# A two-layer diffusion backbone on one core: one gate job moved to the third feed-forward, the filter network's steps spread from turn 6 on, and two norms turned to columns by scaled x and transposes

## What is computed

```
def modulated_norm(x, g, shift, scale):
    return rms_norm(x, g) * (1 + scale) + shift

def half_step_ffn(x, g_pre, g_post, shift, scale, gate, w_gate, w_up, w_down):
    h = modulated_norm(x, g_pre, shift, scale)
    y = (jax.nn.silu(h @ w_gate) * (h @ w_up)) @ w_down
    return x + FFN_RES * gate * rms_norm(y, g_post)

def hyena_filters(n, w1, b1, w2, b2, w3, b3, w4, freq):
    ...
    hdn = jnp.sin(fr * (z @ w1.astype(f32) + b1.astype(f32)))
    hdn = jnp.sin(fr * (hdn @ w2.astype(f32) + b2.astype(f32)))
    hdn = jnp.sin(fr * (hdn @ w3.astype(f32) + b3.astype(f32)))
    filt = (hdn @ w4.astype(f32)).reshape(n, 2, HY_WIDTH)

def reference(...):
    for i in range(DEPTH):
        m_lat = (jax.nn.silu(c) @ w_mod[i] + b_mod[i]).reshape(b, N_MOD, 1, D_MODEL)
        ...
```

## Time and profile before

| what | value |
|---|---|
| median of 3 runs | 1338.75 us (1336.57 to 1341.46) |
| the profiled execution, its own time | 1343.3 us |
| its span in the trace | 1341.5 us |
| busy PE / DVE / ACT / POOL | 97% / 73% / 47% / 9% |
| mean granted TensorE clock | 0.992 of full speed |
| moved by DMA | 275.12 MB |

### The profile page before, as it was taken

The page is one execution under the profiler, slowest core; times in us unless marked ns, Lnnn a source line. Parts: engine busy times, 40 slices in busy tenths (PEclk is TensorE's granted clock), DMA queues, the critical chain, the costliest instruction groups (busy, mean ns, idle before and its releaser), DMA issues.

```text
span 1341.5 us, 21469 instructions
## 1 busy us (share of the span) xinstructions
PE 1306.6 (97%) x7794; PEld 1125.8 (84%) x7794; DVE 982.1 (73%) x1447; ACT 632.9 (47%) x969; POOL 118.1 (9%) x209
## 2 busy tenths in 40 slices
PE   6899999999999999999999999999999999999997
PEld 3678777887778988789999868999998987989996
DVE  5788777788776776759888778887558797865554
ACT  6632333332376665755444337444447434644443
POOL 3000010111000422011111000110000000000000
PEclk8999999999999999999999989999999999999999
DMA  9555566777655753259888635886653536656652
GB/s 361 186 171 178 199 203 248 254 244 262 227 173 173 204 147 105 79 174 363 292 303 296 198 118 198 309 299 198 189 188 127 158 110 204 236 173 188 183 185 102
DMA packets 76359, 275.12 MB, mean 205 GB/s; under 512 B 9226, under 2 KB 9781, under 8 KB 75712
## 3 DMA queue, kind: packets, MB, share of 16 engines
q1 hardware_dynamic: 52128, 187.00, 42.4%
q0 software_dynamic: 24160, 87.12, 19.0%
HBM read 273.04 MB, written 1.05 MB: 204 GB/s over the span
## 4 chain that ended last, share of the span: by engine, by line
PE 86%; DVE 7%; ACT 3%; DMA 2%; issue 1%; DVEq 0%; SPq 0%; ACTq 0%
PE gu L1671 16%; PE gu L1673 16%; PE gu L1672 16%; PE acc L1732 8%; PE acc L1734 8%; PE acc L1733 8%; DVE wlo_r L1006 2%; PE acc L1721 2%; DMA wlo<-in_wstream_dram 1%; ACT whi L617 1%; PE acc L2017 1%; PE acc L2028 1%; DMA x_lat<-in_x_in_dram 1%; PE acc L1995 1%; PE acc L1996 1%
## 5 line engine op out<-in xcount | busy, mean ns | idle before, releaser
L1671 PE MATMUL gu<-h_hi,whi 128*128 128x256 f32 (+1 forms) x1688 | 518.0, 307 | 4.2 <-DVE h_lo L1131 1.3
L1672 PE MATMUL gu<-h_lo,whi 128*128 128x256 f32 (+1 forms) x1688 | 515.3, 305 | 0.0
L1673 PE MATMUL gu<-h_hi,wlo_r 128*128 128x256 f32 (+1 forms) x1688 | 515.0, 305 | 0.0
L1006 DVE TENSOR_TENSOR wlo_r<-wlo,whi 128x1024 fp32r<-128x1024 f32 x350 | 421.5, 1222 | 100.9 <-ACT whi L617 99.3
L617 ACT ACTIVATE whi<-wlo 128x1024 fp32r<-128x1024 f32 x350 | 360.3, 1049 | 97.8 <-DMA wlo<-in_wstream_dram 97.5
L1671 PEld LDWEIGHTS gu<-h_hi,whi 128*128 128x128 f32 x1688 | 318.8, 189 | 28.6 <-issue 4.0
L1672 PEld LDWEIGHTS gu<-h_lo,whi 128*128 128x128 f32 x1688 | 318.8, 189 | 19.0 <-issue 0.7
L1673 PEld LDWEIGHTS gu<-h_hi,wlo_r 128*128 128x128 f32 x1688 | 319.4, 189 | 15.5
L1023 DVE SCALAR_TENSOR_TENSOR part<-wm,cvec,part 128x512 f32<-128x512 f32 x266 | 199.5, 750 | 6.7
L1732 PE MATMUL acc<-whi,act_hi 128*128 128x512 f32 x440 | 176.7, 402 | 2.5 <-DVE act_lo L1219 2.0
L1734 PE MATMUL acc<-wlo_r,act_hi 128*128 128x512 f32 x440 | 174.9, 397 | 0.0
(11 more groups left out here) (337 smaller groups left out, 1233.2 us busy)
## 6 DMA issues: line engine op xcount, KB each, us to landing
wlo<-in_wstream_dram SPq DMA_DIRECT2D x350, 512.0 KB, 3.6
wm<-in_wmod_dram POOLq DMA_DIRECT2D x132, 512.0 KB, 6.1
area<-in_wmod_dram POOLq DMA_DIRECT2D x11, 512.0 KB, 19.6
z<-in_gate_rows_dram POOLq DMA_DIRECT2D x6, 512.0 KB, 6.7
gate_keep<-in_gate_rows_dram POOLq DMA_DIRECT2D x5, 512.0 KB, 7.1
area<-in_rpb_dram POOLq DMA_DIRECT2D x32, 64.0 KB, 3.6
x_lat<-in_x_in_dram SPq DMA_DIRECT2D x1, 1024.0 KB, 7.5
area<-in_ctx_in_dram SPq DMA_DIRECT2D x1, 1024.0 KB, 8.8
```

Of the source, the lines that this page charges most:

```text
L1006: nc.vector.tensor_tensor(wlo[:, u.base % RING, :], raw[:, u.base % RING, :], whi[:, u.base % RING, :].bitcast(F32), ALU.subtract).then_in ...
L1671: nc.tensor.matmul(out_, w_hi, x_hi, start=start, stop=False, skip_group_check=True)
L1672: nc.tensor.matmul(out_, w_hi, x_lo, start=False, stop=False, skip_group_check=True)
L1673: return nc.tensor.matmul(out_, w_lo, x_hi, start=False, stop=stop, skip_group_check=True)
```

## The change

It has three parts. (1) The two jobs of gate block 2 of layer 1 go from the list of `ffn(1)` to that of `ffn(2)`, with their tile loads on POOL and another slot for a gain. (2) The filter network's steps are set to other places, the first three to turns 6 and 7 instead of 8 and 9, with a table of its own for the sines on ACT; the batch's rows, columns and coefficients move two to four steps back. (3) Norms 3 and 5: DVE scales all of x by 1 / rms into `spare`, PE only transposes, and the columns come one unit later.

```
-        [(1, b, h, LAT) for b in (1, 3, 4, 2) for h in range(2)],
-        [(1, b, h, LAT) for b in (6, 7, 5) for h in range(2)],
+        [(1, b, h, LAT) for b in (1, 3, 4) for h in range(2)],
+        [(1, b, h, LAT) for b in (6, 7, 2, 5) for h in range(2)],
...
-            pool.wait_ge(h_ready, 8 * 5)
-            load_gate(1, 2)
-            load_gain(1, 2)
             with pool.Fori(JOB_L[1] + 1, JOB_L[2] + 1) as l:
                 load_job(l, gemv, steps_before(l))
             pool.wait_ge(h_ready, 8 * 6)
-            load_gate(1, 5)
-            load_gain(1, 5)
+            for b in (2, 5):
+                load_gate(1, b)
+                load_gain(1, b)
...
+                if q in IN_PAIRS:
+                    nc.vector.tensor_scalar(spare[:, t, :], X[NORMS[q][2]][:, t, :], rstd[:, i:i + 1], None,
+                                            ALU.mult).then_inc(diag_done, 1)
+                    return
                 nc.vector.tensor_scalar(diag[:, t, :], ident[:, :], rstd[:, i:i + 1], None, ALU.mult).then_inc(diag_done, 1)
...
+                    if q in IN_PAIRS:
+                        ins = nc.tensor.transpose(columns_of(q, kt)[:, t * P:(t + 1) * P], spare[:, t, kt * P:(kt + 1) * P],
+                                                  ident[:, :])
...
-                if ft == 8:
+                if ft == 9:
...
-                if idx == 8:
+                if idx == 9:
...
-FILTER_AT = [(8, 3), (8, 5), (9, 1), (9, 3), (9, 5), (10, 1), (10, 3)]
+FILTER_AT = [(6, 2), (6, 5), (7, 2), (8, 4), (9, 0), (9, 4), (10, 0)]
+SINE_AT = [(6, 3), (7, 0), (7, 3)]
```

More of the change, by code:

```diff
@@ L75 @@
         + [(l, b, h, LAT) for l, b in ((0, 5), (0, 8), (0, 6), (0, 7), (1, 0)) for h in range(2)],
-        [(1, b, h, LAT) for b in (1, 3, 4, 2) for h in range(2)],
-        [(1, b, h, LAT) for b in (6, 7, 5) for h in range(2)],
+        [(1, b, h, LAT) for b in (1, 3, 4) for h in range(2)],
+        [(1, b, h, LAT) for b in (6, 7, 2, 5) for h in range(2)],
         [(1, 8, h, LAT) for h in range(2)]]
-JOB_0 = [0, 22, 30, 36]
-JOB_L = [AHEAD, 20, 28, 34]
+JOB_0 = [0, 22, 28, 36]
+JOB_L = [AHEAD, 20, 26, 34]
 AHEAD_CHUNKS = 4 * AHEAD
@@ L90 @@
 GATE_JOBS = [job for jobs in JOBS for job in jobs if job[1] in GATE_NORM]
-GATE_SLOT = [0, 1, 0, 0, 0, 0]
+GATE_SLOT = [0, 1, 0, 0, 1, 0]
 COLS_AHEAD = [(0, b, h, s) for b, h in AHEAD_LOADS for s in (LAT, CTX)]
@@ L950, in spectra_norms @@
                 spectrum_out(i + 3)
-            ffn(1, peeled=at_steps([(6, 2)] + FILTER_AT, [lambda: batch_rows(1)] + [lambda l=l: sine(l) for l in range(3)]))
+            ffn(1, peeled=at_steps([(6, 4)] + SINE_AT, [lambda: batch_rows(1)] + [lambda l=l: sine(l) for l in range(3)]))
             load_table(ACT.Sqrt)
@@ L1580, in filter_sums @@
                 assert count[0] == FD_SUM[i]
-            ffn(1, peeled=at_steps([(7, 0)] + FILTER_AT, [lambda: (batch_out(1), norm_coef(9), norm_coef(11))]
+            ffn(1, peeled=at_steps([(7, 4)] + FILTER_AT, [lambda: (batch_out(1), norm_coef(9), norm_coef(11))]
                                    + [lambda l=l: sine_argument(l) for l in range(3)]
@@ L1720, in norm_columns @@
                         pe.wait_ge(xt_copied, kt // 2 + 1)
-                    ins = nc.tensor.matmul(columns_of(q, kt)[:, t * P:(t + 1) * P],
-                                           X[NORMS[q][2]][:, t, kt * P:(kt + 1) * P], diag[:, t, :], start=True, stop=True)
+                    if q in IN_PAIRS:
+                        ins = nc.tensor.transpose(columns_of(q, kt)[:, t * P:(t + 1) * P], spare[:, t, kt * P:(kt + 1) * P],
+                                                  ident[:, :])
+                    else:
+                        ins = nc.tensor.matmul(columns_of(q, kt)[:, t * P:(t + 1) * P],
+                                               X[NORMS[q][2]][:, t, kt * P:(kt + 1) * P], diag[:, t, :], start=True, stop=True)
                     if t == 1 and kt % 2:
@@ L2073, in filter_layer @@
                     pe.wait_ge(filt_in, 16 * 7)
-                    pe.wait_ge(gate_free, 10)
+                    pe.wait_ge(gate_free, 8)
                     w, x_ = fw[E, 0:64], zf[E, :]
@@ L2100, in spectrum @@
                 ins.then_inc(fp, 1)
-            ffn(1, 4, peeled=at_steps([(6, 4)] + FILTER_AT, [lambda: batch_columns(1)]
+            ffn(1, 4, peeled=at_steps([(7, 0)] + FILTER_AT, [lambda: batch_columns(1)]
                                       + [lambda l=l: filter_layer(l) for l in range(3)]
```

## The result

The changed kernel takes 1332.08 us (median of 8 runs, 1328.41 to 1335.48), the kernel before in the same comparison 1339.96 (8 runs). The ratio is 0.9948, with a 95% interval of 0.9934 to 0.9962: 7.0 us faster, 5.1 to 8.8. 1330 was forecast, with 1324 to 1337 as range.

The account below looks back on a forecast made before the run. TensorE's own list, busy 97% of the span, was taken to set the end. Terms -5.7 (filter), -1.7 (norm 3), -2.1 (norm 5), -0.3 and +1.0 (feed-forward starts) sum to -8.8: from 1338.75 to 1330 us, range 1324 to 1337.

Parts of the forecast that it names:

- Filter steps, -5.7: Second feed-forward: sine waits and the clock fall behind them vanish, 5.7 us less; bounds -3.1 and -6.8.
- The rivals' 3.4 us for one fall: Cost assumed for each fall of the granted clock behind the transposes of norms 3 and 5: 3.4 us.
- 1.4 us of change-overs: Second feed-forward: loss spread over the filter network's seven places, some 0.2 us each, expected to stay.
- Norm 3, -1.7: Context stage: transposes instead of float32 products, with no wait around them, save 1.7 us.
- The transposes and the scaled x: Norms 3 and 5: 0.115 us per transpose on TensorE, 0.75 us per scaling of x on DVE.
- Norm 5, -2.1: Projections: DVE's train of steps behind the norm still sets the pace, 2.1 us less; bounds -1.2 and -3.9.
- some 2 us fewer of waits for copies behind the norm: Projections, sign of being right: units 9 to 14 wait some 2 us less for their copies.
- Second feed-forward's start, -0.3: Without 1 MB of tiles at its start, the second feed-forward loses its 0.27 us wait for a late split: -0.3.
- Gate job as such, 0: Two sums on PE and two steps on DVE move from second to third feed-forward at no cost: 0.
- Third feed-forward's start, +1.0: Four tiles, 2 MB, ahead of job 27 delay the third feed-forward by 1.0 us, middle of 0 and 2.
- The rival of DMA's pace in every turn: Third feed-forward: 1.6 us lost in each of eight turns, 12.8 in all, ending at 1341.8; chance 0.05.
- The clock behind transposes: Rival: granted clock falls behind norm 3's or 5's transposes, 3.4 us a fall, giving 1333.4 or 1336.8; chance 0.08.

Follow-up runs that it names:

- p1_gate_alone: The kernel before with only the gate job and its four tiles moved to the third feed-forward: 2.4 us slower than before (0.5 to 4.3).
- e1_filter_old: The changed kernel with the filter network's seven steps back at their old places in turns 8 to 10: 2.4 us faster than before (0.7 to 4.2).
- e7_busy_wait: The kernel before with eight unneeded float32 products ahead of the first output step's wait for the third sine: 2.5 us faster than before (0 to 5.1).
- e6b_tiles_more: The changed kernel with two more unread 512 KB tiles at the third feed-forward's start, repeated with more rounds: 5.5 us faster than before (3.4 to 7.6).
- e3_norms_at_8: The changed kernel with the columns of norms 3 and 5 one unit earlier again, behind unit 8: 3.8 us faster than before (1.6 to 5.9).
- e6_tiles_more: The changed kernel with two more unread 512 KB tiles at the third feed-forward's start, first run: 7.9 us faster than before (5.2 to 10.6).
- e2_filter_wide: The kernel before with the filter steps spread a little within turns 8 to 10, gate job and norms unmoved: 4.3 us faster than before (2.5 to 6.0).
- e5_tiles_later: The changed kernel with the third feed-forward's four gate tiles spread over POOL's queue: 9.6 us faster than before (7.5 to 11.9).

## Why the prediction came out as it did

The forecast was 1330 us and 8.8 us less than before; measured were 1332.08 and 7.0 or 6.0 less. Of the 2.1 us between the two medians 1.2 are the starting point: the three runs that it was taken from had a median of 1338.75, the eight of the comparison 1339.96. The rest is in the terms, some of which missed in opposite directions.

**Filter steps, -5.7: right in the mechanism, too large by about a quarter.** The traces of before and after give 5.7. But its 3.4 us for the clock came from one execution; the two others with the same unfilled gap lost 1.8. Against `p1_gate_alone` the filter steps give 209.34 - 205.26 = 4.1, and `e1_filter_old` in the times 2.4 against 7.0 and 6.0, so 3.6 to 4.6. The term that was too large is the clock's. The rivals' 3.4 us for one fall have the same fault. The 1.4 us of change-overs that I kept stayed: 4.1 is what the two waits, 2.3, and the fall, 1.8, make together.

**Norm 3, -1.7:** 1.8 measured. **The transposes and the scaled x:** 0.11 us for a transpose and 0.75 for a scaled x, as worked out from the earlier trace rows.

**Norm 5, -2.1:** 2.3 measured, and the nearness is in part luck. The train behind the norm did not set the pace as forecast: of the 2.2 us that it cost, 1.7 went, so with the shorter norm 3.5 were gained, close to the bound of -3.9 for a train that closes up. What I missed is in front: moving the norm took away the cover of unit 9's wait for a bank, the scaled x made that wait longer, and 1.2 us were lost there. The prediction looked for waits behind the norm alone. Its sign, some 2 us fewer of waits for copies behind the norm, did not come: the brackets fell from 1.17 to 0.23.

**Second feed-forward's start, -0.3:** 0.5, a bracket of 0.27 taken as its price. **Gate job as such, 0:** its sums cost the same in either place, 0.94 us.

**Third feed-forward's start, +1.0 as the middle of 0 and 2: the term that was mis-sized.** It was 2.7, outside these bounds. The step that failed is the bound, "the same lateness costs the fourth 1.70 with two tiles": I took the bracket in the timeline as the whole price, which was 1.98 already in that row, and counted one stop. Here two splits were late, with brackets of 0.13 and 2.06 and costs of 0.40 and 2.33. With 0.2 that the gate steps cost more there than in the second one, this is where 1.9 of the forecast gain went. It is also one of the signs of being wrong that the prediction named, a split in turn 1 over 2 us late, and it came in the profile of the changed kernel. The range had been worked out with +0.5 and +1.5 for this term, narrower than the bounds of 0 and 2. The rival of DMA's pace in every turn is refuted: behind turn 1 nothing is late.

**The clock behind transposes:** no fall at either norm, 1.00 in both windows. The Trainium skill ("TensorE: Matmul & The Clock Gate", Part 4: PE-mode transpose) says that they do not count as busy in the way that matmuls do; over 1.67 us the trace shows nothing of it, and no run here had a longer piece. In `e7_busy_wait` 1.95 us of plain products in float32 were followed by a clock of 1.00, where the empty wait was followed by a fall.

So the sum of what the traces of all runs show is about -4.1 (filter), -1.8, -2.3, -0.5, +2.7 and +0.2 for gate steps: -5.8, beside -7.0 and -6.0 in the times; with the 3.4 us of the one execution before for the clock it is -7.4. The forecast of -8.8 had the clock's price and the turn's price each wrong by 1.6 to 1.7 us, in the same direction.

**Open:** why the clock stayed at its lower level longer behind the same gap in one execution than in two others (3.4 against 1.8 us lost); whether a third MB at the start of the third feed-forward costs anything; and what else makes turn 1 of the fourth late.

## What to carry to other kernels

Before work is moved to make room, look whether the room was short: here a gap of one column unit more between a layer and its sine did it alone, and moving the job cost more than it gave. Tiles that are first needed five to eight turns later should not be issued in one piece where the stream must refill: spread behind the job loads, the same four cost nothing. Where a norm or a product moves out of a place, look in both directions for a wait that it covered. And take the price of a stop from the starts of the matmuls around it: in the feed-forwards here it was some 0.27 us more than the bracket, four times out of four.

## What was not expected of the hardware

A wait of 1.9 us for the third sine was followed by a fall of the granted clock in each of the three profiles that had it (0.69, 0.82 and 0.82 over the stretch behind). For the late split of turn 1 in the third and the fourth feed-forward it went either way. A fall came behind waits of 1.98, 2.05 and 2.37 us in the third (`e6b_tiles_more`, `e3_norms_at_8`, `e6_tiles_more`) and of 1.77, 1.79 and 2.11 in the fourth (`e6b_tiles_more`, `e2_filter_wide`, `e6_tiles_more`). None came behind 2.06 in the third and 1.88 in the fourth of the changed kernel, 1.79 in `e5_tiles_later` and 1.70 in before, nor behind any shorter one between 65 and 1320 us. So the length of a wait alone does not tell whether a fall follows, and two profiles can differ by it where their code does not: `e2_filter_wide` and both runs with more tiles have 1.6 to 1.9 us more than before behind the third feed-forward. And the executions differ at their start: with a clock of 0.91 in the first 60 us they came to the context stage at 382.4 to 382.9 us, with 0.97 at 378.9 to 380.2, and the one with 1.00 at 377.1. That is up to 5.8 us for the same work, as much as the largest part of this change.
